# Layer 0 of a three-block transformer kernel: one weight's low part ahead of the rotation of the scan's inputs, and the exponential and sines ahead of the first weight's high part

## The reference, cut to what matters

```
xn = rms_norm(h, attn_norm_g[layer])
proj = xn @ w_in[layer]
u_ssm, u_g, v_g, q, k, v = jnp.split(proj, [o1, o2, o3, o4, o5], axis=-1)
y_ssm = s5_mixer(u_ssm, ...)
y_sgu = spatial_gating(u_g, v_g, ...)
y_diff = diff_attention(q, k, v, ...)
mixed = jnp.concatenate([y_ssm, y_sgu, y_diff], axis=-1)
h = h + mixed @ w_out[layer]
```

## Time and profile before

| what | value |
|---|---|
| median of three runs | 991.44 us (990.45 to 991.54) |
| profiled execution | 992.79 us, its span 991.0 us |
| TensorE busy | 966.5 us (98%) |
| VectorE busy | 696.4 us (70%) |
| ScalarE busy | 547.1 us (55%) |
| GpSimd busy | 258.1 us (26%) |
| mean granted TensorE clock | 0.993 |

### The profile page before, as it was taken

One profiled execution on the slowest core, in us unless ns is written; L12 is line 12 of the kernel. 1 busy time (PEld: TensorE's weight loads), 2 busy tenths in 40 slices (PEclk: granted clock), 3 DMA queues, 4 the chain that ended last, 5 costly groups with the idle time before them and its releaser, 6 DMA issues.

```text
span 991.0 us, 15869 instructions
## 1 busy us (share of the span) xinstructions
PE 966.5 (98%) x6191; PEld 849.8 (86%) x6191; DVE 696.4 (70%) x1072; ACT 547.1 (55%) x898; POOL 258.1 (26%) x196
## 2 busy tenths in 40 slices
PE   5999999999999999999999999999999999999997
PEld 4878889999978887899999988899877789888886
DVE  5999557778864688586777764558576755666785
ACT  6746646665744655755666554454454454555723
POOL 4891101667800021200445510003122300000030
PEclk9989999999999999999999999999999999999999
DMA  7622255665665552446656566565544445754452
GB/s 280 223 93 86 86 175 188 192 191 172 191 179 162 170 171 85 149 151 200 186 182 187 191 191 192 181 205 178 164 150 149 143 150 162 210 162 152 148 188 84
DMA packets 48474, 165.97 MB, mean 167 GB/s; under 512 B 6544, under 2 KB 7056, under 8 KB 48400
## 3 DMA queue, kind: packets, MB, share of 16 engines
q1 hardware_dynamic: 48400, 164.95, 53.3%
HBM read 162.83 MB, written 1.05 MB: 165 GB/s over the span
## 4 chain that ended last, share of the span: by engine, by line
PE 86%; DVE 9%; ACT 2%; issue 1%; DMA 1%; POOL 0%; SPq 0%; DVEq 0%; POOLq 0%; ACTq 0%
PE PJ L595 13%; PE PJ L597 13%; PE PJ L596 13%; PE PJ L590 10%; PE PJ L588 10%; PE PJ L589 10%; DVE wlo L1699 3%; PE PJ L551 2%; PE PJ L552 2%; PE PJ L553 2%; DMA raw<-weights_in 1%; PE T L1032 1%; PE PJ L712 1%; PE T L1023 1%; ACT whi L1091 1%
## 5 line engine op out<-in xcount | busy, mean ns | idle before, releaser
L1699 DVE TENSOR_TENSOR wlo<-raw,whi 128x1024 fp32r<-128x1024 f32 x294 | 371.2, 1293 | 97.7 <-ACT whi L1091 95.3
L1091 ACT ACTIVATE whi<-raw 128x1024 fp32r<-128x1024 f32 x294 | 303.3, 1062 | 78.5 <-DMA raw<-weights_in 68.7
L588 PE MATMUL PJ<-xthb,whi 128*128 128x256 f32 x864 | 243.0, 281 | 0.9 <-DVE wlo L1699 0.5
L590 PE MATMUL PJ<-xthb,wlo 128*128 128x256 f32 x864 | 242.3, 280 | 0.0
L589 PE MATMUL PJ<-xtlb,whi 128*128 128x256 f32 x864 | 241.4, 279 | 0.0
L595 PE MATMUL PJ<-whi,xthb 128*128 128x512 f32 (+1 forms) x432 | 176.0, 407 | 2.6 <-DVE wlo L1699 2.2
L596 PE MATMUL PJ<-wlo,xthb 128*128 128x512 f32 (+1 forms) x432 | 168.8, 391 | 0.0
L597 PE MATMUL PJ<-whi,xtlb 128*128 128x512 f32 (+1 forms) x432 | 168.7, 390 | 0.0
L588 PEld LDWEIGHTS PJ<-xthb,whi 128*128 128x128 f32 x864 | 163.0, 189 | 1.7 <-issue 1.5
L589 PEld LDWEIGHTS PJ<-xtlb,whi 128*128 128x128 f32 x864 | 163.0, 189 | 0.2
L590 PEld LDWEIGHTS PJ<-xthb,wlo 128*128 128x128 f32 x864 | 162.9, 189 | 0.0
(11 more groups left out here) (398 smaller groups left out, 1358.2 us busy)
## 6 DMA issues: line engine op xcount, KB each, us to landing
raw<-weights_in SPq DMA_DIRECT2D x294, 512.0 KB, 3.5
rt<-bmerge_in SPq DMA_DIRECT2D x6, 256.0 KB, 4.2
xres<-x_in SPq DMA_DIRECT2D x2, 512.0 KB, 5.9
memx<-mem_in SPq DMA_DIRECT2D x2, 512.0 KB, 4.0
y_out<-xn SPq DMA_DIRECT2D x4, 256.0 KB, 2.4
rowv<-rows_in SPq DMA_DIRECT2D x1, 576.0 KB, 11.1
ptmp<-bexp_in SPq DMA_DIRECT2D x2, 256.0 KB, 6.9
cex<-cexp_in SPq DMA_DIRECT2D x2, 256.0 KB, 9.0
```

What stands on the lines that cost most here:

```text
L588: pe.matmul(o, a, xh[:, k, :], start=(first and f % 2 == 0), stop=False, skip_group_check=True)
L590: m = pe.matmul(o, b, xh[:, k, :], start=False, stop=last, skip_group_check=True)
L1091: act.activation(whi[:, p % HIGHS, :], raw[:, p % LOADS, :], ACT.Copy).then_inc(hi_ready, 1)
L1699: dve.tensor_tensor(wlo[:, p % LOADS, :], raw[:, p % LOADS, :], whi[:, p % HIGHS, :].bitcast(F32), ALU.subtract).then_inc(lo_ready, 1)
```

## The change

On ScalarE, in the very first norm, the high part of the first weight (`hi_upto(1)`) goes behind the exponential and the two sines instead of ahead of them. On VectorE, in layer 0 alone, the call of `lo_upto` ahead of the rotation of the scan's inputs goes one pair further, so that the low part of pair 14 is made ahead of the rotation and not behind it. Nothing else changes: no wait, buffer or transfer is added or removed.

```
@@ ScalarE, before the layers
             for half in range(2):
                 squares(0, xres, 0, half)
-            hi_upto(1)
             act.wait_ge(sem("par_ready"), 2)
             act.activation(sp_[:, 3, :], sp_[:, 1, :], ACT.Exp).then_inc(sem("par_a"), 1)
             act.activation(sp_[:, 6, :], sp_[:, 5, :], ACT.Sin).then_inc(sem("par_a"), 1)
             act.activation(sp_[:, 7, :], sp_[:, 5, :], ACT.Sin, scale=0.5).then_inc(sem("par_a"), 1)
+            hi_upto(1)
             norm_hi(0, 0)
@@ VectorE, in the loop over the layers
-                lo_upto(s0 + (17 if l else 14))
+                lo_upto(s0 + (17 if l else 15))
```

## The result

The changed kernel takes 994.02 us (median of six, 993.39 to 995.09) against 991.33 for the kernel before (990.19 to 991.54): a ratio of 1.0029, 95% interval 1.0017 to 1.0040. It is 2.7 us slower, inside the range given and above the 993.0 forecast. The profiled execution took 993.39, the lowest of the six, its span 991.6.

What follows compares the result with a forecast made beforehand. TensorE was taken to bound the kernel, VectorE the stretch up to pair 15. Minus 1.5, plus 1.35 and plus 1.7 make plus 1.55 us, from median 991.44 to 993.0; range 990.2 to 995.0.

Steps and rivals of the forecast that it cites:

- Bound: Whole kernel: TensorE bounds, 86% of the chain; VectorE holds it from 22.24 to 76.94 us; later work only shifts.
- Part 1, the mechanism: ScalarE's start: exponential, table load and sines, 1.74 us, fit into the idle time before weight 0 lands; GpSimd moves up too.
- D: Rival at ScalarE's start: the table switch needs about 1.4 us beyond its load, delaying the first high part; 994.1, chance 0.03.
- Part 1, the size: ScalarE's start: first matmul 1.6 us earlier, passed on through VectorE and GpSimd; taken as minus 1.5 us.
- Part 2, VectorE's order: VectorE, layer 0: taking turns with GpSimd at SBUF holds L1840, pair 15's low part comes later; plus 1.35 us.
- C: Rival on VectorE: pair 14 straight behind pair 13 keeps the port, one turn less waited for; 988.6, chance 0.09.
- Part 2, the clock: TensorE before pair 15: one hole of 5 us, then slow clock on pair 15 and toeplitz products; plus 1.7 us.
- A: Rival on TensorE after the hole: the clock costs nothing or little; minus 0.15 us, 991.3, chance 0.26.
- B: Rival on TensorE after the hole: the clock stays low for 6.8 us of work; plus 3.25 us, 994.7, chance 0.16.
- The sum: Whole kernel: minus 1.5, plus 1.35, plus 1.7 gives plus 1.55 us; this forecast had chance 0.46.

Runs made afterwards that it cites:

- e1: The kernel before with only the ScalarE edit (exponential and sines ahead of the first high part), VectorE's order as before: 990.99 us, ratio 1.0000.
- e10: The kernel before with x's second tile loaded ahead of weight 0, so that weight 0 lands later: 993.43 us, ratio 1.0021.
- e11: The kernel before with the ScalarE edit alone and x's second tile loaded ahead of weight 0, so that it lands later: 991.59 us, ratio 1.0006.
- e5: The kernel before, unchanged, profiled a second time: 991.23 us.
- e2: The kernel before with only the VectorE edit (pair 14's low part ahead of the rotation), ScalarE's order as before: 994.33 us, ratio 1.0030.

## Why the prediction was right or wrong

**Bound.** Right in the main: up to pair 15's low part VectorE sets the pace, then TensorE, and a difference at 80 us comes out at the end to within 0.8 us, save for the loss at 405. But in e1 and in the second trace of before, TensorE had the chain from pair 14 on.

**Part 1, the mechanism: right.** The 1.74 us fit ahead of the first high part, the table load took 1.28 and brought no drain (D is out), GpSimd's chain came along.

**Part 1, the size: wrong, and it is the step that failed.** The term of minus 1.5 was measured at minus 0.2 by the medians (e1 against before; the ratio is 1.0000, with an interval of about 0.9 us either way). It took weight 0's landing at 8.61 as a property of the kernel. In the old order norm_hi starts some 2.7 us after the landing, in the new one at about 9.5; so part 1 is worth what the weight lands after 6.8 us, and it usually lands at 6.6 to 7.9. Worked out from the twelve landings, that is an estimate of 0.5 us in the mean, and 1.8 us in the first trace. The prediction had the hint: the profiled execution stood 1.35 above the median. By the two traces of before, the late weight is 1.05 of it at the toeplitz products (79.92 against 78.87), and 0.5 more are lost between 290 and 390 us. The prediction took from the median a loss that the median did not contain. With the weight made late (e10, e11), part 1 does give 1.8 us by the medians and 1.2 by the traces.

**Part 2, VectorE's order: right**, plus 1.35 forecast and 1.4 measured (13.0 against 14.5 us from pair 13 to pair 15, nothing without output_powers). L1840 was held as foreseen; C is out.

**Part 2, the clock: right in what happens, too large as a difference.** The hole, the fall and 3.4 us of slow work on pair 15 came, and 1.6 us are won where the hole is filled. But plus 1.7 was counted against an old order whose slow stretch was hidden, and that too was a property of the one execution: in e1 and e5 the old order has a slow stretch of 6.8 us of its own and loses 0.6 to 0.8 us of the chain to it. What the new order adds is the 4.7 us (after) against the 3.7 (e1), or the 5.2 (e2) against the 3.9 (e5): 1.0 to 1.3. A is out. B's 6.8 us of slow clock did come (73.0 to 79.9), but half of it lay in the hole.

**The sum.** In the traces part 2 moves the toeplitz products by 2.3 us (after against e1) and by 2.9 (e2 against e5): 1.3 and 1.6 of VectorE's order, 1.0 and 1.3 of the clock. The medians give 3.0 and 3.1. The rest, up to 0.7, is not explained; the six executions of the changed kernel alone lie 1.7 us apart, and the profiled one is the lowest. The forecast of plus 1.55 was short because part 1 gave 1.3 us less than it took off, while the clock's term was some 0.5 too large. That 994.02 lies in the range is in part luck: the range reached up to 995.0 for the milder half of rival B, a longer slow stretch on the chain, and not for a part 1 that is worth nothing. The number is even nearer to B's 994.7 than to 993.0, without B's mechanism.

## What to carry to other kernels

Before a gain is read from a wait for a transfer, compare the profiled execution with the median of the runs; if it is slower by about as much as the gain, the wait may be that execution's, and a second trace costs little. The same holds for a cost that one trace shows as hidden: the slow stretch was off the chain in the first trace of before and on it in the second. Moving an instruction to where it seems free can still cost when another engine shares its port: put instructions that read PSUM beside the other engine's long SBUF products, and look at what then falls to instructions that had slipped through. Work done early for TensorE is no gain while a later input is the late one; it gathers the idle time into one hole, and more of the clock's fall then lands on the chain.

## What the runs showed of the hardware that had not been expected

Two identical launches differ by up to 2 us in when the first weight lands (6.63 and 8.61 us after the start, both in the kernel before).

Two executions of the same kernel also differ in where the clock is low: 52.6 to 59.3 and 73.0 to 76.4 in the first trace of before, 69.6 to 76.4 in the second.

Seventeen or more added matmuls, which were over before 80 us, cost TensorE 0.8 to 1.2 us at 405 to 422 us, in four kernels of four, where four transfers are issued in a row. In three of them one transfer lands 2.3 to 2.5 us after its predecessor instead of 1.3, because one of its 16 parts is late; why that part is late stays open. A small edit can thus move a measurement of 0.1% far from where it was made.
